# The second phase of a hybrid layer in 27 stages per block: HGRN2, Mamba-2 and the dense products in a new order

## The reference

```python
mod = c_act @ w_ada + b_ada                      # six vectors sh1, sc1, g1, sh2, sc2, g2
h   = rmsnorm(x, g_norm1) * (1 + sc1) + sh1
proj = h @ w_in                                  # HGRN2 | Mamba-2 | RWKV-7 inputs
o_hg = hgrn2_chunked(...);  y_mb = ssd_chunked(...);  o_rw = rwkv7_scan(...)
x = x + g1 * (concat(o_hg, y_mb, o_rw) @ w_out)
h = rmsnorm(x, g_norm2) * (1 + sc2) + sh2
x = x + g2 * ((silu(h @ w_gate) * (h @ w_up)) @ w_down)     # D_FF = 2816
y = rmsnorm(x, g_final)
```

## Time and profile before

| | |
|---|---|
| times of three runs | 1790.70, 1798.88, 1802.05 us |
| median | 1798.88 us |
| span of the profiled execution | 1790.1 us |
| lowest of the three times, beside that span | 0.6 us above it |
| second phase up to its joint | 609.3 to some 1046 us |
| busy over the whole span | PE 1594.7, DVE 1043.3, ACT 660.4, POOL 249.0 us |

### The profile page before, as it was taken

One profiled execution on the slowest core, in us unless ns is written; L12 is line 12 of the kernel. 1 busy time (PEld: TensorE's weight loads), 2 busy tenths in 40 slices (PEclk: granted clock), 3 DMA queues, 4 the chain that ended last, 5 costly groups with the idle time before them and its releaser, 6 DMA issues.

```text
span 1790.1 us, 32642 instructions
## 1 busy us (share of the span) xinstructions
PE 1594.7 (89%) x13639; PEld 1451.0 (81%) x13639; DVE 1043.3 (58%) x2152; ACT 660.4 (37%) x1133; POOL 249.0 (14%) x331
## 2 busy tenths in 40 slices
PE   4799999889999677777888899989899999999997
PEld 2798888778887443575777899988899999999997
DVE  5513456868554556676765254676665566655554
ACT  2323333223432322343433254343544444433333
POOL 4421111111111200231334300100000000000000
PEclk9899999889999667897998999999999999999999
DMA  8111001101112244321132434544464544564552
GB/s 320 53 48 36 25 25 37 44 33 50 49 43 106 80 164 151 110 86 34 42 89 71 136 117 130 151 121 138 119 200 137 160 122 139 152 176 137 145 151 75
DMA packets 276684, 188.09 MB, mean 105 GB/s; under 512 B 7880, under 2 KB 264377, under 8 KB 275513
## 3 DMA queue, kind: packets, MB, share of 16 engines
q1 hardware_dynamic: 266050, 160.28, 29.8%
q0 software_dynamic: 7536, 22.47, 3.8%
q10 hardware_dynamic: 2950, 3.24, 0.5%
HBM read 172.82 MB, written 13.18 MB: 104 GB/s over the span
## 4 chain that ended last, share of the span: by engine, by line
PE 70%; DVE 17%; ACT 7%; issue 3%; DMA 1%; SPq 0%; POOL 0%; DVEq 0%; ACTq 0%; POOLq 0%
PE bank L1346 16%; PE bank L1347 16%; PE bank L1348 16%; PE bank L1282 3%; PE bank L1368 3%; PE bank L1369 2%; ACT WHI L1959 2%; PE bank L1370 2%; DVE WLO L2442 1%; PE bank L1512 1%; PE bank L1520 1%; PE bank L1522 1%; PE bank L1697 1%; PE bank L1456 1%; PE bank L1377 1%
## 5 line engine op out<-in xcount | busy, mean ns | idle before, releaser
L2442 DVE TENSOR_TENSOR WLO<-RAW,WHI 128x1024 fp32r<-128x1024 f32 (+4 forms) x235 | 247.1, 1052 | 265.1 <-ACT WHI L1959 263.3
L1959 ACT CAST WHI<-RAW 128x1024 fp32r<-128x1024 f32 (+4 forms) x294 | 266.4, 910 | 227.6 <-PE bank L1348 201.0
L1346 PE MATMUL bank<-HAH,WHI 128*128 128x384 f32 (+1 forms) x832 | 277.2, 333 | 12.4 <-DVE HAL L2625 5.9
L1347 PE MATMUL bank<-HAL,WHI 128*128 128x384 f32 (+1 forms) x832 | 273.7, 329 | 0.0
L1348 PE MATMUL bank<-HAH,WLO 128*128 128x384 f32 (+1 forms) x832 | 273.0, 328 | 0.0
L1346 PE MATMUL bank<-MIXR,WHI 128*128 128x384 f32 (+2 forms) x528 | 174.1, 330 | 12.6 <-DVE MIXR L2572 3.8
L1093 POOL TENSOR_TENSOR WLO<-RAW,WHI 128x1024 fp32r<-128x1024 f32 (+1 forms) x59 | 124.6, 2114 | 434.7 <-ACT WHI L1959 434.7
L1346 PEld LDWEIGHTS bank<-HAH,WHI 128*128 128x128 f32 x832 | 159.9, 192 | 16.3 <-issue 15.5
L1347 PE MATMUL bank<-MIXR,WHI 128*128 128x384 f32 (+2 forms) x528 | 171.1, 324 | 0.0
L1348 PE MATMUL bank<-MIXR,WLO 128*128 128x384 f32 (+2 forms) x528 | 171.1, 324 | 0.0
L1347 PEld LDWEIGHTS bank<-HAL,WHI 128*128 128x128 f32 x832 | 159.9, 192 | 0.1
(11 more groups left out here) (582 smaller groups left out, 3031.6 us busy)
## 6 DMA issues: line engine op xcount, KB each, us to landing
RAW<-in_w_gate SPq DMA_DIRECT2D x66, 512.0 KB, 3.8
RAW<-in_w_up SPq DMA_DIRECT2D x66, 512.0 KB, 3.8
RAW<-in_w_ada SPq DMA_DIRECT2D x32, 512.0 KB, 4.4
RAW<-in_w_in SPq DMA_DIRECT2D x26, 512.0 KB, 3.8
RAW<-in_w_out SPq DMA_DIRECT2D x24, 512.0 KB, 3.5
RAW<-in_w_down SPq DMA_DIRECT2D x32, 384.0 KB, 3.1
RAW<-in_w_down SPq DMA_DIRECT2D x32, 320.0 KB, 2.8
ADAW<-in_w_ada SPq DMA_DIRECT2D x8, 1024.0 KB, 19.8
```

The source lines that it names most:

```text
L1346: mm(bank[:, 0:w], whi[:, k, :], hi_k, start=(k == 0), stop=False)
L1347: mm(bank[:, 0:w], whi[:, k, :], lo_k, start=False, stop=False)
L1959: a.copy(w_split(i)[0][:, 0:nk, :], RAW[u % NRAW][:, 0:nk, :]).then_inc(w_hi, 1)
L2442: v.tensor_tensor(wlo[:, 0:nk, :], RAW[u % NRAW][:, 0:nk, :], whi[:, 0:nk, :].bitcast(F32), ALU.subtract).then_inc(w_lo, 1)
```

## The change

The eight rounds get an order in which every item holds one step of the data's flow: 27 stages per block, the tail of block b-1 (`mb_ssq`, `mb_S`, `hg_out`, `mb_out`) within round b, and HGRN2's decays for b+1 and b+2 (`hg_nabs`, `hg_soft`) in it as well. To cut the items, some semaphores are split: Mamba's log decays, SEG and MM move to the counters of its front part, `nabs` gets one of its own. `turn` and `att` are two items, the modulation's copy, transposes and sum (`adc`, `adt`, `adm`) as well. Three tables hold the order: AROUND for blocks 0 to 2 (thirteen places for an ada product), FROUND for the others, with places for one dense unit (two halves) behind `hg_turn`, `mb_acum`, `hg_state`, two behind `hg_ssq` and one behind `hg_rs`, and NROUND for block 4, where the norm of chunk 0 is spread: `sum` behind the fills of `mb_acum`, `scaled` 0 behind `mb_m`, `scaled` 1 behind `hg_o`, `head` behind `hg_ssq`, `rest` 0 behind `hg_high`, `rest` 1 behind `mb_y`. Before, the norm's items came from `fill` in block 4, separated by pauses. The transposes of x in blocks 0 to 2 go to banks 2 and 7 instead of 0 and 1, and the first dense units wait for their copies. The number of dense units in front of `join` stays the same.

```diff
-HGF_DVE = ['nabs', 'logf', 'diffs', 'factors']
+HGF_DVE = ['logf', 'diffs', 'factors']
-MBF_DVE = ['xdt', 'cb']
-MB_DVE = ['seg', 'm', 'y', 'S', 'z', 'out']
-MB_PE = ['acum', 'y', 'S', 'ssq']
-MB_ACT = ['E2', 'L', 'squared', 'rs']
+MBF_DVE = ['xdt', 'cb', 'seg', 'm']
+MBF_PE = ['turned', 'acum']
+MBF_ACT = ['E2', 'L']
+MB_DVE = ['y', 'z', 'S', 'out']
+MB_PE = ['y', 'S', 'ssq']
+MB_ACT = ['squared', 'rs']
...
+        def x_banks(i):
+
+            if i < 9:
+                return BK8[3 + 2 * (i % 2)], BK8[4 + 2 * (i % 2)]
+            return (BK8[2], BK8[7]) if i < 12 else (BK8[0], BK8[1])
...
-        NOW = {('out', (0, KT - 1)): [('sum', 3), ('pause', 0), ('scaled', (3, 0)), ('scaled', (3, 1)), ('head', 3),
-                                      ('pause', 0), ('rest', (3, 0)), ('rest', (3, 1)), ('pause', 0)]}
+        NOW = {('out', (0, KT - 1)): [('stop', 0)]}
...
-        FILL = {'hg_att': 2, 'mb_decay': 2, 'hg_o': 2, 'mb_prod': 2, 'mb_turn': 2, 'hg_levels': 2}
-        for b in range(NB):
-            items = [('hg_att', b), ('hg_state', b), ('mb_decay', b), ('hg_o', b), ('hg_logits', b + 1), ('mb_prod', b),
-                     ('hg_sq', b), ('hg_gate', b + 1), ('hg_low', b + 1), ('hg_high', b + 1), ('mb_turn', b + 1), ('mb_sq', b), ('hg_out', b),
-                     ('hg_levels', b + 1), ('mb_out', b), ('hg_x', b)]
...
+        AROUND = [('mb_ssq', -1), ('mb_S', -1), ('mb_turn', 0), ('ada', 0), ('hg_levels', 0), ('hg_turn', 0), ('ada', 0),
+                  ('hg_att', 0), ('ada', 0), ('mb_xd', 0), ('hg_out', -1), ('mb_out', -1), ('ada', 0), ('hg_mask', 0),
+                  ('ada', 0), ('mb_acum', 0), ('ada', 0), ('mb_seg', 0), ('mb_L', 0), ('hg_state', 0), ('ada', 0), ('mb_m', 0),
+                  ('hg_o', 0), ('ada', 0), ('hg_gate', 1), ('hg_low', 1), ('hg_x', 0), ('mb_prod', 0), ('ada', 0), ('hg_ho', 0),
+                  ('hg_ssq', 0), ('ada', 0), ('hg_high', 1), ('ada', 0), ('hg_nabs', 2), ('mb_y', 0), ('mb_sq', 0), ('ada', 0),
+                  ('hg_rs', 0), ('ada', 0), ('hg_soft', 2)]
+        FROUND = [('mb_ssq', -1), ('mb_S', -1), ('mb_turn', 0), ('hg_levels', 0), ('hg_turn', 0), ('fill', 2), ('hg_att', 0),
+                  ('mb_xd', 0), ('hg_out', -1), ('mb_out', -1), ('hg_mask', 0), ('mb_acum', 0), ('fill', 2), ('mb_seg', 0),
+                  ('mb_L', 0), ('hg_state', 0), ('fill', 2), ('mb_m', 0), ('hg_o', 0), ('hg_gate', 1), ('hg_low', 1),
+                  ('mb_prod', 0), ('hg_ho', 0), ('hg_ssq', 0), ('fill', 2), ('fill', 2), ('hg_high', 1), ('hg_nabs', 2),
+                  ('mb_y', 0), ('mb_sq', 0), ('hg_rs', 0), ('fill', 2), ('hg_soft', 2)]
+        NROUND = [('mb_ssq', -1), ('mb_S', -1), ('mb_turn', 0), ('hg_levels', 0), ('hg_turn', 0), ('fill', 2), ('hg_att', 0),
+                  ('fill', 2), ('mb_xd', 0), ('hg_out', -1), ('mb_out', -1), ('hg_mask', 0), ('mb_acum', 0), ('fill', 2),
+                  ('sum', 0), ('mb_seg', 0), ('mb_L', 0), ('hg_state', 0), ('mb_m', 0), ('scaled', 0), ('hg_o', 0),
+                  ('scaled', 1), ('hg_gate', 1), ('hg_low', 1), ('mb_prod', 0), ('hg_ho', 0), ('hg_ssq', 0), ('head', 0),
+                  ('hg_high', 1), ('rest', 0), ('hg_nabs', 2), ('mb_y', 0), ('rest', 1), ('go', 0), ('mb_sq', 0), ('hg_rs', 0),
+                  ('fill', 2), ('hg_soft', 2)]
...
+        def ada_quantum():
+
+            if late and not turning:
+                group, part, half = UNITS[QUANTA[late[0]][0]][1]
+                PLAN2.append(('mm', late.pop(0)))
+                if (part, half) == (KT - 1, 1):
+                    turning.extend([[3, ('adc', group)], [4, ('adt', group)], [9, ('adm', group)]])
...
+                if QP2 <= q < QJ and PREV[q] is None and half != 1:
+                    pe.wait_ge(x_act, 12)
+                    pe.wait_ge(x_dve, 12)
...
-                    if 0 < b <= 3:
-                        pe.wait_ge(x_act, 9 + b)
-                        pe.wait_ge(x_dve, 9 + b)
...
+                elif stage == 'att':
+                    if b:
+                        pe.wait_ge(hg_act, step(HG_ACT, 'rs', b - 1))
...
                 elif stage == 'x':
-                    pe.wait_ge(*V('out'))
-                    pe.wait_ge(mb_act, step(MB_ACT, 'rs', b))
                     turn_x(9 + b, XTOK2)
...
                     if arg == 0:
+                        act.wait_ge(hg_dve, step(HG_DVE, 'out', 2))
+                        act.wait_ge(mb_dve, step(MB_DVE, 'out', 2))
                         act.wait_ge(ada_turned, 3)
```

More of the change, by code:

```diff
@@ new lines, in kernel_program, with turn_group @@
+        turning = []
+        def turn_group():
+            for due in turning:
+                due[0] -= 1
+            while turning and turning[0][0] <= 0:
+                PLAN2.append(turning.pop(0)[1])
+        def ada_quantum():
[4 more added lines that the diff above has]
+                    turning.extend([[3, ('adc', group)], [4, ('adt', group)], [9, ('adm', group)]])
@@ new lines, in kernel_program @@
+        PLAN2 += [('hg_nabs', 1), ('hg_soft', 1)]
+        for b in range(NB + 1):
+            for stage, ahead in (AROUND if b < 3 else NROUND if b == 4 else FROUND):
+                at = b + ahead
+                if stage == 'ada':
+                    ada_quantum()
+                elif stage == 'fill':
+                    if b < NB and ('mb_out', 2) in PLAN2:
+                        fill(ahead)
+                elif stage in ('sum', 'head'):
+                    fill(len(QUANTA))
+                    PLAN2.append((stage, 3))
+                elif stage in ('scaled', 'rest'):
+                    PLAN2.append((stage, (3, ahead)))
+                elif stage == 'go':
+                    assert ffn[0][0] == 'stop', ffn[0]
+                    ffn.pop(0)
+                elif 0 <= at < NB and (stage, at) != ('hg_levels', 0):
+                    PLAN2.append((stage, at))
+                    turn_group()
@@ L1674, in hg @@
                 HB = HB2[b % 2]
-                if stage == 'att':
+                if stage == 'turn':
                     pe.wait_ge(hgf_dve, step(HGF_DVE, 'factors', b))
@@ L1750, in mb @@
                     mm(M2[:, 0:P], XB[4][64:P, t_], XB[5][64:P, t_], start=True, stop=True).then_inc(mbf_pe, 1)
-                elif stage == 'decay':
+                elif stage == 'acum':
                     pe.wait_ge(mbf_dve, step(MBF_DVE, 'cb', b))
@@ L2253, in T_ @@
                     return hg_pe, step(HG_PE, name, b)
-                if stage == 'logits':
-                    act.wait_ge(hgf_dve, step(HGF_DVE, 'nabs', b))
+                if stage == 'soft':
+                    act.wait_ge(hgn_dve, b + 1)
                     tables(LN_EXP)
@@ L2266, in hg @@
                     a.activation(HD[:, :, :, :], HD[:, :, :, :], ACT.Exp).then_inc(hgf_act, 1)
-                elif stage == 'att':
+                elif stage == 'turn':
                     act.wait_ge(*T_('turned'))
@@ L2313, in T_ @@
                     return mb_pe, step(MB_PE, name, b)
-                if stage == 'decay':
-                    act.wait_ge(*T_('acum'))
+                if stage == 'acum':
+                    act.wait_ge(mbf_pe, step(MBF_PE, 'acum', b))
                     for gr in range(2):
@@ L2319, in mb @@
                                             ACT.Exp)
-                    last.then_inc(mb_act, 1)
-                    act.wait_ge(*V('seg'))
-                    a.activation(SEG[:, :, :], SEG[:, :, :], ACT.Exp).then_inc(mb_act, 1)
+                    last.then_inc(mbf_act, 1)
+                elif stage == 'L':
+                    act.wait_ge(mbf_dve, step(MBF_DVE, 'seg', b))
+                    a.activation(SEG[:, :, :], SEG[:, :, :], ACT.Exp).then_inc(mbf_act, 1)
                 elif stage == 'sq':
@@ L2387, in _ @@
             for what, arg in PLAN2:
[L2388 removed]
+                if what == 'adc':
                     ada_act(arg)
@@ L2983, in hg @@
                     v.tensor_tensor(HQ[:, :, :], HB[:, 0:2, :], HX[:, :, :], ALU.mult).then_inc(hgf_dve, 1)
-                elif stage == 'att':
+                elif stage == 'mask':
                     dve.wait_ge(*T_('att'))
@@ L3075, in mb @@
                 cols = slice(b * BLK, (b + 1) * BLK)
-                if stage == 'turn':
-                    dve.wait_ge(mbf_pe, b + 1)
+                if stage == 'xd':
+                    dve.wait_ge(mbf_pe, step(MBF_PE, 'turned', b))
                     if b:
@@ L3084, in mb @@
                     v.tensor_tensor(CBM[:, 1, :], M2[:, 0:P], triu[:, :], ALU.mult).then_inc(mbf_dve, 1)
-                elif stage == 'decay':
-                    dve.wait_ge(*A('E2'))
+                elif stage == 'seg':
+                    dve.wait_ge(mbf_act, step(MBF_ACT, 'E2', b))
                     for h in range(8):
@@ L3089, in mb @@
                                                ACOL[:, b, h:h + 1], 0.0, ALU.subtract, ALU.min)
-                    last.then_inc(mb_dve, 1)
-                    dve.wait_ge(*A('L'))
```

(3 more changed lines are left out.)

62 lines of the change are left out of this document (24 added, 38 removed).

## The result

The changed kernel takes 1808.22 us (median of five runs, 1807.33 to 1813.27) against 1798.88 us: a ratio of 1.0071, with a 95% interval of 1.0049 to 1.0092. It is 0.7% slower, and 47 us above the 1761 of the forecast; the range, 1730 to 1789, does not hold it. The profiled execution has a span of 1805.6 us against 1790.1, so 15.5 us of difference where the medians show 9.3. Profiles tell the places, medians the size.

The account below looks back on a forecast made before the run. PE's time was taken as the bound: 354.7 us busy and 86 idle in seven stretches. Terms 88 + 34.5 + 52 + 46.5 + 48.8 + 48 + 84.5 = 402.3 us against 440.7, 38 less, gave 1761 us; range 1730 to 1789.

Parts of the forecast that it names:

- I count 5 us of waits for each: Products 5 to 6 and 6 to 7: PE waits 5 us in each, giving 48.8 and 48 us.
- the slower rival: Dense blocks: up evictions hold DVE, 63 us a stretch instead of 52; 1817 us in all, chance 0.07.
- Against: such a hold is there today: Argument against the slower rival: block 5 already has such a hold, and few PE waits there exceed 4.9 us.
- 76 + 3 + 9: Start to product 2: PE busy 76, more ada products 3, remaining waits 9 (3 a block, mostly HSH); 88 us.
- no change in what matters: First two stretches stay within 10 us because ada loads limit PE, whose waits only move; 1790 us, chance 0.10.
- the busy time of PE from product 2 on: Stretches from product 2: PE busy 27, 47 and 36.7 us, then as many dense units as before (43.3, 43.7).
- the wait at the norm: Product 4 to 5: of PE's 9.0 us wait some 8 us is left, behind HT instead of ahead.
- the first dense unit's wait: Product 2 to 3: PE waits about 6 us for HAL, the split of the mixed input.
- MM's waits turned into HSH's: Sign in the modulation blocks: PE's waits for the mask product MM become waits for HSH, 3 us a block mostly.
- The gap between the halves of the attention: Start to product 2: the 3.3 us PE wait between the attention halves goes, as ACT's HKT copy is hidden.
- less: Only modulation blocks gain; POOL's splits block DVE, 7 us more in each of three dense stretches; 1782 us, chance 0.18.
- More: Dense blocks fill up too, 42 us each for two stretches, PE waiting only at the norm; 1738 us, chance 0.20.

Follow-up runs that it names:

- e9_out_only: Changed kernel, eviction of the unit before put ahead of the next weight's split for output-projection units alone (blocks 3 and 4); 1805.22 us (1.0046).
- e4_behind_y: Changed kernel, pair of dense units in blocks 3 and 5 to 7 placed behind high, nabs, y and the square; 1806.55 us (1.0058).
- b1_copy_first: Kernel before the change, eviction of the unit before put ahead of the next weight's split up to the joint; 1785.48 us (0.9932).
- small loads: Changed kernel, modulation weight loads cut to 32 KB instead of 512 from the fourth tile on, outputs not the reference's; 1795.07 us (0.9992).
- the exchange: Changed kernel, eviction of the unit before put ahead of the next weight's split on all engines up to the joint; 1771.28 us (0.9862).
- e10_all_behind_y: Changed kernel with the exchange, seven buffers for modulation weights, and the dense pair behind high, nabs, y and the square; 1756.97 us (0.9785).
- the two repairs: The exchange and seven buffers for modulation weights, on the changed kernel; with the dense pair moved as in e10_all_behind_y, 1756.97 us.
- the two halves of the exchange: Changed kernel, eviction ahead of split for output-projection units alone, 1805.22 us (1.0046), or for up units alone, 1791.97 us (0.9975).

## Why the prediction was wrong

The forecast was 51.1 us too low by stretch: 12.1 in the first, 1.9 in the second, 37.1 from product 3 to the joint. Two steps failed.

*The holds by evictions (37 us), the larger.* The step is "I count 5 us of waits for each", in products 5 to 7, with nothing for it in the other stretches. The mechanism was named, from the 6.98 us of the earlier trace rows, and its worst case was the slower rival at 63 us a stretch with 0.07. Measured were 61.4, 52.9, 57.1 and 54.2, in sum 225.6, just under the 232 (four times 58) from which I had let that rival decide. Three things were missing. First, in the out blocks the same split stands ahead of ACT's square of the evicted tile, which costs 8.0 us in the third stretch by `e9_out_only`; I had looked at up products alone, and not at the gate units either. Second, the length: the split waits for a unit that PE may not have begun. In the old order the longest wait for MIXR was 5.2 us, in the new one 12.1, and in the rows of block 5 above it is the product and the sum of squares that PE does before it comes to the unit, at a granted clock of 0.50 from 857.2 to 864.1 us. That length is not the whole price: `e4_behind_y` brought the longest wait for MIXR to 5.9 us and gained nothing. I had carried the old length into the new order. Third, the clock: of the 37 us some 14 are products that ran at 1.2 instead of 2.4 GHz, in an order in which PE was idle more. "Against: such a hold is there today" was no argument against: `b1_copy_first` shows that it cost 13 us today.

*The loads (12 us in this profile, 17 on the average of 105.0).* The step is the sum of the first stretch, 76 + 3 + 9, so 79 busy and 9 idle: it has no term for the weights of the modulation, which took 12.5 us of PE's time, though the rival "no change in what matters" had named them with 0.10 on the grounds of a DMA share of 0.51. With small loads the stretch is 89.2 us and with seven buffers 92.4, where 88 were forecast. The share was the wrong row to judge by. Four products stand in a row behind the sum of squares and only three buffers are there; that could be counted in the table of the change. In blocks 0 and 1 the third and the fourth product of that row wait 2.30, 1.44, 2.10 and 2.59 us, 8.4 of the 12.5. The waits for HSH, 10.3 us in 3, are the 9 that I had set. That the miss of 12.1 us and the loads' 12.5 agree is chance: the idle time was 28.9 us instead of 9, with 5.3 us without a releaser among it, and the busy time 71.2 instead of 79 (76.5 on average). That the two repaired stretches come near 88 is in part the same luck: they hold 16.8 and 20.6 us of idle time, not 9, beside 72.4 and 71.8 busy.

What held: the busy time of PE from product 2 on, within some 4 us a stretch (24.4, 49.9, 38.3, 47.4 and 44.5 us against 27, 47, 36.7, and 43 to 44 twice); the wait at the norm of some 8 us (7.2 for HAL); the first dense unit's wait (8.1 for the weight, with HAL 8.6 right behind it, against 6); the clock of the first stretch above 0.80 (0.84, though down to 0.75 in other profiles of that order); nothing behind the joint; MM's waits turned into HSH's. The gap between the halves of the attention did not go wholly: two waits of 2.05 and 2.24 us without a cause in the profile are left. Three terms were added up slightly wrong (36.7 + 8 + 2 is 46.7 and not 46.5, and with 5 us each the two stretches from product 5 to 7 come to 48.3 and 48.7, not 48.8 and 48); the sum is the same within 0.4 us.

Of the other rivals, "less" (POOL's splits block DVE) is not the cause. DVE's busy time from product 3 to the joint rose by 7.1 us (189.8 against 182.7), of 21 us in that rival, and with the exchange it is 184.2. The stretching itself is real: the product to MIXR at 872.30 took 2.46 us beside a split of POOL,

```profile
871.93 2.41 POOL L1137 TENSOR_TENSOR WLO<-RAW,WHI 128x1024 fp32r<-128x1024 f32 x1 [15.68 <-ACT WHI L2002]
```

and on average 1382 ns in the changed kernel (1298 ns in the one before). Its place beside the split is made by the order: the copy comes right behind the split on ACT, so that DVE's product and POOL's rest start within 0.4 us of each other. With the exchange it takes 712 ns, and some steps of `high` are stretched in its place (their mean goes from 404 and 406 to 647 and 527 ns). The Trainium skill (SBUF — State Buffer, section Who interferes with whom) says that a DVE instruction with two SBUF inputs contends with a GpSimd instruction that reads SBUF, and calls the shared ports an exclusive lock. These rows agree: the product ends 0.4 us after the split. But the rise of 7 us in DVE's busy time is far from the 37 in question. How much such stretching adds to PE's waits at single places, as at the sum of squares above, stays open.

"More" was below the truth of the repaired kernels as well: `e10_all_behind_y` reaches 1757. That this is near the forecast of 1761 doesn't make the forecast right, since that was given for the kernel without these repairs. It shows, though, that both gaps are found, since with the two repairs and the pair of units behind `mb_sq` the stretches take 92.3, 35.3, 52.4, 45.9, 44.3, 47.6 and 87.7 us where 88, 34.5, 52, 46.5, 48.8, 48 and 91.0 were forecast.

Open is the wait of an ada product without a releaser, near 695 us in the changed kernel, 2.5 to 5.6 us in all profiles of these modulation blocks, which stays with seven buffers. That the gate units make up what the two halves of the exchange leave over is not shown either.

## What to carry to other kernels

Where two steps share a queue, look for the one that waits for work not yet begun: a refill of a double buffer (here the weight split) must stand behind all that others wait for, such as the tail of an eviction. That was worth 13, 24 and 37 us in three orders of the same work. A new order is priced with the waits that it makes, not with those of the old one. For prefetched operands, count the longest run of their users against the number of buffers before trusting the mean share of the DMA engines: here it was 0.58 with three buffers, where PE waited, and 0.52 with seven, where it did not.

## What was not expected of the hardware

The first stretch of one and the same order with three buffers took from 100.1 to 109.6 us in seven profiles, and the difference is not in the waits, which were 27.1 to 30.3 us, but in the busy time of the same products, 71.2 to 81.5 us at a granted clock of 0.84 to 0.75. With seven buffers three profiles lie within 92.2 to 92.4 us. And idle time of PE is paid twice: in the five dense stretches the exchange took away 22.7 us of idle time and, with the granted clock that rose, 14.4 us of busy time. In the kernel before, the same exchange took 3.4 us of idle time and 9.3 us of busy time (238.6 instead of 247.9, the clock 0.92 instead of 0.89), so the second price is no fixed part of the first.
